# The last layer norm of an encoder layer: what POOL did is shared out between ACT and DVE

## What is computed

```python
def layer_norm(x, g, b):
    xf = x.astype(F32)
    mu = jnp.mean(xf, axis=-1, keepdims=True)
    var = jnp.mean(jnp.square(xf - mu), axis=-1, keepdims=True)
    return ((xf - mu) * lax.rsqrt(var + LN_EPS) * g.astype(F32) + b.astype(F32)).astype(x.dtype)

def encoder_layer(x, ...):
    ...
    x = layer_norm(ALPHA * x + merged @ w_out, ln1_g, ln1_b)
    moe = hierarchical_moe(x, w_route_group, b_route_group, w_route_expert, b_route_expert,
                           w_expert_in, w_expert_out)
    return layer_norm(ALPHA * x + moe, ln2_g, ln2_b)
```

## Time and profile before

| | us |
|---|---|
| median of 3 runs | 1547.08 |
| lowest and highest | 1546.88, 1547.58 |
| profiled execution, its own time | 1546.55 |
| its span, first to last instruction | 1544.8 |
| last norm, from the first load's issue to the span's end | 1494.32 to 1544.8 |

### The profile page before, as it was taken

The page is one execution under the profiler, slowest core; times in us unless marked ns, Lnnn a source line. Parts: engine busy times, 40 slices in busy tenths (PEclk is TensorE's granted clock), DMA queues, the critical chain, the costliest instruction groups (busy, mean ns, idle before and its releaser), DMA issues.

```text
span 1544.8 us, 21064 instructions
## 1 busy us (share of the span) xinstructions
PE 1332.0 (86%) x7598; PEld 1129.0 (73%) x7599; DVE 759.1 (49%) x1000; ACT 621.3 (40%) x709; POOL 334.0 (22%) x319
## 2 busy tenths in 40 slices
PE   3999999999997899999999997138899999899940
PEld 1889878888796788977888897136688778778830
DVE  2332355321642432355421463618865766875548
ACT  2332444332313322254422222327755664874521
POOL 1232000000302043000000112443523532653214
PEclk9999999999995799999999997559999999999975
DMA  7944400034462344310024431749977977997233
GB/s 165 261 90 101 91 1 1 1 82 137 109 164 111 83 92 100 83 28 1 1 59 128 114 83 74 258 135 302 350 256 230 320 240 256 323 345 249 78 118 142
DMA packets 161418, 222.49 MB, mean 144 GB/s; under 512 B 20775, under 2 KB 136103, under 8 KB 160535
## 3 DMA queue, kind: packets, MB, share of 16 engines
q1 hardware_dynamic: 137296, 177.40, 39.5%
q0 software_dynamic: 12800, 34.74, 8.1%
q10 hardware_dynamic: 11244, 9.29, 1.9%
HBM read 200.14 MB, written 34.35 MB: 152 GB/s over the span
## 4 chain that ended last, share of the span: by engine, by line
issue 56%; PE 19%; POOL 8%; DMA 7%; DVE 5%; ACT 2%; ACTq 2%; SPq 0%; POOLq 0%; DVEq 0%
PE banks L645 5%; PE banks L647 5%; PE banks L646 5%; DMA moe_raw<-in_w_expert_in 2%; POOL gated L534 1%; POOL pt L510 1%; DMA moe_raw<-in_w_expert_out 1%; POOL prob L517 1%; POOL slots L550 1%; ACTq L1000 1%; PE banks L871 1%; DMA toeplitz_rows<-bias_rows 1%; DVE moe_lo L1552 1%; PE banks L893 1%; ACT moe_hi L1163 1%
## 5 line engine op out<-in xcount | busy, mean ns | idle before, releaser
L1552 DVE TENSOR_TENSOR moe_lo<-moe_raw,moe_hi 128x2048 fp32r<-128x2048 f32 x102 | 233.1, 2289 | 75.6 <-ACT moe_hi L1163 75.5
L1163 ACT ACTIVATE moe_hi<-moe_raw 128x2048 fp32r<-128x2048 f32 x102 | 195.0, 1915 | 65.1 <-PE banks L647 37.4
L1269 DVE TENSOR_TENSOR wlo<-raw,whi 128x2048 fp32r<-128x2048 f32 (+1 forms) x56 | 125.2, 2236 | 182.7 <-ACT whi L1022 182.7
L645 PE MATMUL banks<-wlo,xT 128*128 128x256 f32 x640 | 183.5, 287 | 7.7 <-DVE xT L1379 4.5
L646 PE MATMUL banks<-whi,xT 128*128 128x256 f32 x640 | 182.6, 285 | 0.0
L647 PE MATMUL banks<-whi,xT 128*128 128x256 f32 x640 | 182.5, 285 | 0.0
L645 PE MATMUL banks<-xT,whi 128*128 128x512 f32 x448 | 174.7, 390 | 0.0
L646 PE MATMUL banks<-xT,whi 128*128 128x512 f32 x448 | 174.4, 389 | 0.0
L647 PE MATMUL banks<-xT,wlo 128*128 128x512 f32 x448 | 174.3, 389 | 0.0
L1022 ACT ACTIVATE whi<-raw 128x2048 fp32r<-128x2048 f32 (+1 forms) x56 | 103.5, 1849 | 120.8 <-PE banks L647 120.8
L645 PE MATMUL banks<-moe_lo,xeh 128*128 128x512 f32 x368 | 147.1, 400 | 5.7 <-DVE xel L1558 4.3
(11 more groups left out here) (222 smaller groups left out, 2330.5 us busy)
## 6 DMA issues: line engine op xcount, KB each, us to landing
moe_raw<-in_w_expert_in SPq DMA_DIRECT2D x128, 512.0 KB
raw<-in_w_in SPq DMA_DIRECT2D x80, 512.0 KB, 6.4
moe_raw<-in_w_expert_out SPq DMA_DIRECT2D x64, 512.0 KB
raw<-in_w_out SPq DMA_DIRECT2D x16, 512.0 KB, 5.5
toeplitz_rows<-bias_rows POOLq DMA_DIRECT2D x4, 1152.0 KB, 12.7
kqv<-in_x SPq DMA_DIRECT2D x8, 512.0 KB, 9.4
pt<-in_x SPq DMA_DIRECT2D x2, 2048.0 KB, 9.1
raw<-in_w_branch_a SPq DMA_DIRECT2D x8, 512.0 KB, 6.2
```

Source lines behind the costliest of these rows:

```text
L645: mm(dst, left[0], right[1], start=first, stop=False)
L1163: A(moe_hi[m % SPLIT_E], moe_raw[m % RAW_E], ACT.Copy).then_inc(e_hi, 1)
L1269: V.tensor_tensor(view(wlo[c % 2], shape), view(raw[c % 2], shape), view(whi[c % 2], shape).bitcast(F32), ALU.subtract).then_inc(w_split, 1)
L1552: V.tensor_tensor(moe_lo[m % SPLIT_E], moe_raw[m % RAW_E], moe_hi[m % SPLIT_E].bitcast(F32), ALU.subtract).then_inc(e_lo, 1)
```

## The change

Three things change, all in the last norm. POOL does nothing in it any more, and DVE does the two wide operations for all eight tiles; they now add a negated mean, `fin_neg`, where they subtracted a mean. For six tiles, `ACT_TILES = (1, 2, 4, 5, 6, 7)`, DVE's statistics are gone: ACT makes a Copy pass over the tile into a scratch tile whose only use is the sum of each row, a small Copy that turns the sum into the negated mean, and a Square pass with that as its bias, which again sums each row. DVE divides by 1024 and adds epsilon. Tiles 0 and 3 keep `bn_stats` on DVE, with one small operation more for the negated mean. And ACT's program is in another order: the root of tile j - 1 stands behind the passes of tile j.

```diff
--- before.py
+++ after.py
@@ -152,7 +152,7 @@
 HALVES = 2
 HW = DE // HALVES
 CONSTS = 16 * 13
-POOL_TILES = (1, 4, 6)
+ACT_TILES = (1, 2, 4, 5, 6, 7)
 RAW_E, SPLIT_E = 4, 6
 
 
@@ -306,7 +306,8 @@
         sum_tile = [place(f"sum_tile{j}", D) for j in range(NT)]
         ln2p = place("ln2p", 2 * D)
         fin_stats = place("fin_stats", NT * 16)
-        fin_mv, fin_scale, fin_shift = place("fin_mv", NT * 2), place("fin_scale", NT), place("fin_shift", NT)
+        fin_mv, fin_scale, fin_neg = place("fin_mv", NT * 2), place("fin_scale", NT), place("fin_neg", NT)
+        fin_scratch = place("fin_scratch", D)
 
 
         ident_in, sel_in, rope_in, const_in = sem("ident_in"), sem("sel_in"), sem("rope_in"), sem("const_in")
@@ -351,9 +352,8 @@
         y_act, y_dve = sem("y_act"), sem("y_dve")
         y_out = [sem(f"y_out{i}") for i in range(2)]
         sum_in = [sem(f"sum_in{i}") for i in range(NT)]
-        f_step, f_var, f_root, f_scale, f_normed, f_gained, f_ready, f_last, f_out = [
-            sem(n) for n in ("f_step", "f_var", "f_root", "f_scale", "f_normed", "f_gained", "f_ready", "f_last",
-                           "f_out")]
+        f_step, f_sum, f_mean, f_square, f_var, f_root, f_last, f_out = [
+            sem(n) for n in ("f_step", "f_sum", "f_mean", "f_square", "f_var", "f_root", "f_last", "f_out")]
 
         by_name = {"q_copied": q_copied, "va_ready": va_ready, "b_act": b_act, "b_dve": b_dve,
                    "gate_ready": gate_ready, "yb_used": yb_used, "ya_used": ya_used, "residual": residual, "xlo": xlo,
@@ -463,10 +463,7 @@
                     sp.dma_start(ln2p[:, 0:D], ln2_g[0].partition_broadcast(P)).then_inc(ln2_in, 16)
                     sp.dma_start(ln2p[:, D:2 * D], ln2_b[0].partition_broadcast(P)).then_inc(ln2_in, 16)
             for j in range(NT):
-                if j in POOL_TILES:
-                    sp.wait_ge(f_ready, POOL_TILES.index(j) + 1)
-                else:
-                    sp.wait_ge(f_last, j - sum(i < j for i in POOL_TILES) + 1)
+                sp.wait_ge(f_last, j + 1)
                 sp.dma_start(out_v[j // TT, :, j % TT], sum_tile[j]).then_inc(f_out, 16)
             sp.wait_ge(f_out, 16 * NT)
 
@@ -627,13 +624,6 @@
                 pool.wait_ge(n, passes * (NE // 2) * 16 + 16)
             nc.gpsimd.tensor_tensor(wait_bearer[:, 1:2], wait_bearer[:, 0:1], wait_bearer[:, 0:1], ALU.add) \
                 .then_inc(experts_pool, 1)
-
-            pool.wait_ge(ln2_in, 32)
-            for n, j in enumerate(POOL_TILES):
-                pool.wait_ge(f_normed, n + 1)
-                nc.gpsimd.tensor_tensor(sum_tile[j], sum_tile[j], ln2p[:, 0:D], ALU.mult).then_inc(f_gained, 1)
-                pool.wait_ge(f_gained, n + 1)
-                nc.gpsimd.tensor_tensor(sum_tile[j], sum_tile[j], ln2p[:, D:2 * D], ALU.add).then_inc(f_ready, 1)
 
 
         @block.tensor
@@ -1206,13 +1196,26 @@
                             A(y_sb[b][:, d * 512:(d + 1) * 512], bank[4 + d][:, :], ACT.Copy, scale=slot_gate(b, 0)).then_inc(y_act, 1)
                         e_split(pair, b * ECH + XCH + 1 + SPLIT_E)
 
-            for j in range(NT):
+            act.wait_ge(experts_dve, 1)
+
+            def root(j):
                 act.wait_ge(f_var, j + 1)
                 A(fin_scale[:, j:j + 1], fin_scale[:, j:j + 1], ACT.Sqrt).then_inc(f_root, 1)
-                if j in POOL_TILES:
-                    act.wait_ge(f_scale, POOL_TILES.index(j) + 1)
-                    A(sum_tile[j], sum_tile[j], ACT.Identity, bias=fin_shift[:, j:j + 1], scale=fin_scale[:, j:j + 1]) \
-                        .then_inc(f_normed, 1)
+
+            for j in range(NT + 1):
+                if j in ACT_TILES:
+                    n = ACT_TILES.index(j) + 1
+                    mean, total, square = fin_mv[:, 2 * j:2 * j + 1], fin_mv[:, 2 * j + 1:2 * j + 2], fin_scale[:, j:j + 1]
+                    act.wait_ge(sum_in[j], 16)
+                    if n > 1:
+                        act.wait_ge(f_square, n - 1)
+                    A(fin_scratch, sum_tile[j], ACT.Copy, accum_out=total).then_inc(f_sum, 1)
+                    act.wait_ge(f_sum, n)
+                    A(fin_neg[:, j:j + 1], total, ACT.Copy, scale=-1.0 / D).then_inc(f_mean, 1)
+                    act.wait_ge(f_mean, n)
+                    A(fin_scratch, sum_tile[j], ACT.Square, bias=fin_neg[:, j:j + 1], accum_out=square).then_inc(f_square, 1)
+                if j >= 1:
+                    root(j - 1)
 
 
         @block.vector
@@ -1606,24 +1609,26 @@
             chain.sem = f_step
 
             def moments(j):
+                scale = fin_scale[:, j:j + 1]
+                if j in ACT_TILES:
+                    dve.wait_ge(f_square, ACT_TILES.index(j) + 1)
+                    V.tensor_scalar(scale, scale, 1.0 / D, LN_EPS / ALPHA ** 2, ALU.mult, ALU.add).then_inc(f_var, 1)
+                    return
                 st = fin_stats[:, 16 * j:16 * j + 12]
                 dve.wait_ge(sum_in[j], 16)
                 for f in range(2):
                     ins = V.bn_stats(st[:, 6 * f:6 * f + 6], sum_tile[j][:, f * 512:(f + 1) * 512])
                 chain(ins)
                 chain(V.bn_aggr(fin_mv[:, 2 * j:2 * j + 2], st))
-                V.tensor_scalar(fin_scale[:, j:j + 1], fin_mv[:, 2 * j + 1:2 * j + 2], LN_EPS / ALPHA ** 2, None, ALU.add) \
-                    .then_inc(f_var, 1)
+                V.tensor_scalar(fin_neg[:, j:j + 1], fin_mv[:, 2 * j:2 * j + 1], -1.0, None, ALU.mult)
+                V.tensor_scalar(scale, fin_mv[:, 2 * j + 1:2 * j + 2], LN_EPS / ALPHA ** 2, None, ALU.add).then_inc(f_var, 1)
 
             def normalise(j):
-                cx, mean, scale = sum_tile[j], fin_mv[:, 2 * j:2 * j + 1], fin_scale[:, j:j + 1]
+                cx, scale = sum_tile[j], fin_scale[:, j:j + 1]
                 dve.wait_ge(f_root, j + 1)
                 chain(V.reciprocal(scale, scale))
-                if j in POOL_TILES:
-                    V.scalar_tensor_tensor(fin_shift[:, j:j + 1], mean, -1.0, scale, ALU.mult, ALU.mult).then_inc(f_scale, 1)
-                    return
                 dve.wait_ge(ln2_in, 32)
-                chain(V.scalar_tensor_tensor(cx, cx, mean, ln2p[:, 0:D], ALU.subtract, ALU.mult))
+                chain(V.scalar_tensor_tensor(cx, cx, fin_neg[:, j:j + 1], ln2p[:, 0:D], ALU.add, ALU.mult))
                 V.scalar_tensor_tensor(cx, cx, scale, ln2p[:, D:2 * D], ALU.mult, ALU.add).then_inc(f_last, 1)
 
             moments(0)
```

## The result

| | before | changed |
|---|---|---|
| median, us (runs) | 1546.31 (6) | 1532.18 (6) |
| lowest and highest | 1541.92, 1547.58 | 1527.65, 1537.66 |
| profiled execution, its own time | 1546.55 | 1527.65 |
| its span | 1544.8 | 1526.0 |

The ratio of the mean times is 0.9916, 95% interval 0.9888 to 0.9943: 13 us less, between 9 and 17. The runs of both kernels now spread over 6 and 10 us, where the three shown before lay within 0.7. The changed kernel's profiled execution is the fastest of its six.

A forecast was written before the change was run, and what follows sets the result against it. DVE was taken to bound the last norm, slowed by turns with POOL. 2.78 - 7.54 - 5.43 = -10.2 us took the profiled 1546.55 to 1536.35, as a median 1536.9 us; range 1535.3 to 1539.6.

The forecast's parts named there:

- about 0.5 us of scatter and gaps: Whole run: allowance that, with the doubled table load, widened the forecast to the range of 1535.3 to 1539.6 us.
- It stood 0.5 below the median, so as a median I say 1536.9: Whole run: profiled execution forecast at 1536.35 us, raised to a median because the earlier profiled execution lay below its median.
- The sum, 10.2: Last norm: 2.78 us later start, 7.54 less for DVE's later moments, 5.43 less for its normalising; 10.2 saved.
- The start of tile 0's reciprocal: Last norm, after tile 1's squares, table load and root: about 1507.28 instead of 1504.50, 2.78 us later.
- the eight times 2.71: Last norm: DVE normalises all eight tiles at 2.71 us each, the last 2.79, together 21.76, 5.43 less than before.
- DVE bounds the norm, ACT stays ahead: Last norm: ACT's squares ready some 2 us before DVE asks, tiles 4 to 7; ACT bounds only from 3.37 per tile.
- Two signs that the prediction named: Profile after, last norm: ACT passes at 1.26 and 1.35 us; DVE idle about 6 us before tile 0's reciprocal.
- The table load on the path: Last norm, between tile 1's Square and tile 0's root: DVE waits for the load, charged 1.30 us.
- The doubled load: Last norm, first root: a switch cost seen only when waited for adds a second 1.28 us, giving 1538.2; chance 0.07.
- Summing halves ACT's rate: Last norm, ACT: a summing pass takes two passes' time, 4.68 us per tile; run 1544.7 us; chance 0.03.
- Slower, it was not POOL: Last norm: any engine streaming a sum tile slows DVE's wide operations, about 1.9 us per hit; 1560 us; chance 0.02.
- Something else that keeps DVE slow: Last norm: DVE stays slow for a cause other than POOL, anywhere from 1534 to 1547 us; chance 0.06.

The follow-up runs named there:

- the early load: Changed kernel plus a one-column root that nobody reads, ahead of tile 1's passes, so the table load runs early: norm 38.10 us, 1.6 less.
- the other load order: Changed kernel with tile 1's statistics on DVE and tile 1's load ahead of the gains and shifts: norm 36.68 us, ratio 0.99.

## Why the prediction was wrong, point by point

**The step that failed** is the term for all that the change doesn't touch: "about 0.5 us of scatter and gaps", on top of a starting value taken from three runs and one profile. Single runs spread with a standard deviation of 2.9 us. The first load of the norm, and with it the end of the untouched part, differs by 4.4 us between two executions of the kernel before, and by 8.0 over the ten profiles. The three runs lay within 0.7 us and were high together: their median of 1547.08 stands 3.1 above the mean of 63. The step "It stood 0.5 below the median, so as a median I say 1536.9" thus started 3 us too high. For the same reason "About 3.1 us (0.2%) is what a measurement of this kernel can tell from no change" doesn't hold for a few runs: it is one standard deviation of a single one. From the mean, the same sum gives 1544.0 - 10.2 = 1533.8, and with 10.76 for the norm 1533.2. The six runs of the result have a mean of 1532.5, all 12 of the changed kernel 1532.3. Of the 4.7 us between 1536.9 and the median of 1532.18, the starting value makes 3.1, the sum 0.6, and the last 1.0 is within the scatter of six runs. The sum was right within 0.6; its starting value and its margin were not.

**The sum, 10.2, measured 10.76.** The start of tile 0's reciprocal was to be 4.42 after tile 1's landing and is 4.21: each of the two sums adds 0.1 and not 0.20, since the readout overlaps its pass, and a tile takes ACT 2.66 and not 2.87. At tile 2 DVE was to lose 0.31 and, ACT being that much quicker, lost nothing (1501.85, 1501.91). The last store ends 3.09 after DVE, not 3.27. Against that, tile 1 landed 8.64 after the first issue and not 8.54 as before. Together 0.21 + 0.31 + 0.18 - 0.10 = 0.60, of 0.56. Tile 3's statistics, the eight times 2.71 and the 1.28 came as said.

**DVE bounds the norm, ACT stays ahead:** right. DVE asked for tile 4's squares at 1509.02 and they had been there since 1504.78; from tile 2 on ACT waited for DVE (2.9 us in two roots, 1.6 in a third), never DVE for ACT. Two signs that the prediction named came otherwise. ACT's passes stand at 1.04 to 1.06 and 1.15 with readouts of 0.19 beside them, not at 1.26 and 1.35. And DVE's two waits before tile 0's reciprocal are 7.0 us together, not about 6.

**The table load on the path:** right; taken off the path it gave 1.40, for a forecast of 1.30.

**The rivals.** The doubled load: out by the rows and the early load. Summing halves ACT's rate: out, a pass with a sum is as long as one without, with 186 ns of readout. Slower, it was not POOL: out. The wide operations ran at 1.28 with ACT's passes beside them, 1499.33 beside 1499.00, and went back to over 3 when POOL was made to work. Something else that keeps DVE slow: out, none of the sixteen is above 1285 ns. The Trainium skill, "SBUF — State Buffer", section "Who interferes with whom", gives ACT ports of its own that it shares with no engine. This trace agrees, and for wide DVE operations with two inputs, of which the one before had none beside an ACT pass.

## What to carry to other kernels

Before a gain of under 1% is forecast in us, ask how far the untouched part of the program scatters: a handful of runs that agree within 0.1% may be one draw. Judge such a change by its own stretch in the profiles (here 50.5 to 39.7, each repeated within 0.3), and the whole by means over many runs. And where DVE and POOL both stream tiles with two inputs, giving DVE more work and POOL none can be the faster way, by 5 us here with three tiles more on DVE.

## What the runs showed of the hardware that I had not expected

- PE's granted clock differs from execution to execution of one program: 0.58 and 0.95 in one stretch of 10 us, 0.74 and 1.00 in another, with PE busy for 7.4 to 8.4 us of each. Over whole profiled executions it was 0.934 to 0.942.
- An ACT pass that sums is followed by a readout of 186 ns, of which about 0.09 lies beneath the pass. The Copy pass itself is not slower (1.04 to 1.06, and 1.06 without a sum); the Square pass with its bias took 1.15, as estimated.
- Which of DVE and POOL is held up depends on who starts first: DVE's 1.28 became 3.34 behind POOL, POOL's 2.35 became 3.29 behind DVE. Even a POOL addition of one number per partition, 0.19 by itself (1485.12 in the kernel before), took 2.10 when it came 0.23 behind the start of a wide DVE operation with which it shares no tile (1058.19, behind `moe_lo` at 1057.96).
- A table load that stands first in ACT's work ran at once in the kernel before and waited 13.19 us for its root's input in the kernel with tile 1 on DVE, and 13.13 and 12.92 with all statistics on DVE and with the other load order. One difference in ACT's program is on record: in these three a wait for DVE's end of the expert loop (`experts_dve`) stands ahead of the root's own wait, in the kernel before only the root's own. Whether that is the reason was not tried. A root of one column that nobody reads, with only the first of the two waits ahead of it, made the load early.
